# Reordering the recurrent mixer: solve ahead of the masks, operands of the second pair in the waits of the first, squares bank by bank, a new closing order

## The reference, cut to what matters

```python
def step(state, inp):
    r_t, w_t, k_t, v_t, kk_t, a_t = inp
    sa = jnp.einsum('bhvk,bhk->bhv', state, -kk_t)
    state = (state * w_t[:, :, None, :]
             + sa[..., None] * (kk_t * a_t)[:, :, None, :]
             + v_t[..., None] * k_t[:, :, None, :])
    return state, jnp.einsum('bhvk,bhk->bhv', state, r_t)
...
mean = jnp.mean(y, axis=-1, keepdims=True)
var = jnp.mean(jnp.square(y - mean), axis=-1, keepdims=True)
y = ((y - mean) * lax.rsqrt(var + GN_EPS)).reshape(B, S, RWKV_WIDTH) * ln_w + ln_b
...
y = y + bonus.reshape(B, S, RWKV_WIDTH)
return (y * g).astype(p_r.dtype)
...
x = x + jnp.concatenate([y_rw, y_pool], axis=-1) @ w_out[l]
```

## Time and profile before

| | us |
|---|---|
| median of 3 runs | 1474.83 |
| lowest and highest | 1473.97, 1476.49 |
| the profiled execution | 1472.81 |
| its span | 1471.0 |
| PE busy | 1426.8 (97%) |
| POOL, DVE, ACT busy | 778.8, 537.5, 504.5 |

### The profile page before, as it was taken

The page is one execution under the profiler, slowest core; times in us unless marked ns, Lnnn a source line. Parts: engine busy times, 40 slices in busy tenths (PEclk is TensorE's granted clock), DMA queues, the critical chain, the costliest instruction groups (busy, mean ns, idle before and its releaser), DMA issues.

```text
span 1471.0 us, 21748 instructions
## 1 busy us (share of the span) xinstructions
PE 1426.8 (97%) x8086; PEld 1172.9 (80%) x8086; DVE 537.5 (37%) x732; ACT 504.5 (34%) x709; POOL 778.8 (53%) x1028
## 2 busy tenths in 40 slices
PE   7999999999999999999999999989899999999997
PEld 5787888888888788888888867867688888888887
DVE  6986422222002842222200468964344222221003
ACT  5424433333213433232221466225443233232222
POOL 1663745555555855455555666563465545455553
PEclk9999999999999999999999999999999999999999
DMA  9882432223222322323332232200132322323321
GB/s 363 309 323 96 138 118 95 99 98 99 100 88 84 100 100 91 108 86 99 101 100 88 70 102 72 73 2 4 33 114 98 101 99 91 108 86 100 100 72 58
DMA packets 45705, 156.96 MB, mean 107 GB/s; under 512 B 5328, under 2 KB 8656, under 8 KB 45520
## 3 DMA queue, kind: packets, MB, share of 16 engines
q1 hardware_dynamic: 45648, 156.16, 30.9%
HBM read 154.04 MB, written 2.10 MB: 106 GB/s over the span
## 4 chain that ended last, share of the span: by engine, by line
PE 82%; DVE 10%; ACT 4%; issue 3%; POOL 1%; DMA 0%; DVEq 0%; SPq 0%; POOLq 0%; ACTq 0%
PE ps L1764 26%; PE ps L1766 26%; PE ps L1765 26%; POOL w_lo L543 1%; DVE tri_p L1191 1%; DVE tri_x L1191 1%; PE ps L2221 1%; DVE mid_sq L1194 1%; ACT w_hi L726 1%; DVE pads L1191 0%; DVE f_buf L1191 0%; DVE act_lo L1194 0%; DVE mod_acc L1194 0%; DVE rAR L1191 0%; PE ps L2279 0%
## 5 line engine op out<-in xcount | busy, mean ns | idle before, releaser
L543 POOL TENSOR_TENSOR w_lo<-raw,w_hi 128x256 fp32r<-128x256 f32 x932 | 694.3, 778 | 583.4 <-ACT w_hi L726 583.1
L1764 PE MATMUL ps<-act_hi,w_hi 128*128 128x512 f32 x1328 | 522.6, 393 | 8.2 <-POOL w_lo L543 3.5
L1766 PE MATMUL ps<-act_hi,w_lo 128*128 128x512 f32 x1328 | 517.1, 389 | 0.0
L1765 PE MATMUL ps<-act_lo,w_hi 128*128 128x512 f32 x1328 | 516.8, 389 | 0.0
L726 ACT ACTIVATE w_hi<-raw 128x1024 fp32r<-128x1024 f32 x233 | 244.7, 1054 | 432.8 <-PE ps L1766 402.4
L1764 PEld LDWEIGHTS ps<-act_hi,w_hi 128*128 128x128 f32 x1328 | 249.3, 188 | 67.4 <-POOL w_lo L543 4.8
L1766 PEld LDWEIGHTS ps<-act_hi,w_lo 128*128 128x128 f32 x1328 | 249.2, 188 | 52.3
L1765 PEld LDWEIGHTS ps<-act_lo,w_hi 128*128 128x128 f32 x1328 | 249.4, 188 | 52.0 <-issue 1.4
L1764 PE MATMUL ps<-hid_hi,w_hi 128*128 (+2 forms) x588 | 220.0, 374 | 0.8 <-issue 0.8
L1765 PE MATMUL ps<-hid_lo,w_hi 128*128 (+2 forms) x588 | 219.7, 374 | 0.0
L1766 PE MATMUL ps<-hid_hi,w_lo 128*128 (+2 forms) x588 | 219.7, 374 | 0.0
(11 more groups left out here) (281 smaller groups left out, 989.1 us busy)
## 6 DMA issues: line engine op xcount, KB each, us to landing
raw<-weight_units SPq DMA_DIRECT2D x233, 512.0 KB, 3.5
wm_mid<-mod_units SPq DMA_DIRECT2D x18, 512.0 KB, 8.6
wm_ring<-mod_units SPq DMA_DIRECT2D x14, 512.0 KB, 8.6
wm_early<-mod_units SPq DMA_DIRECT2D x8, 512.0 KB, 7.8
wm_late<-mod_units SPq DMA_DIRECT2D x8, 512.0 KB, 8.0
x_tok<-tokens SPq DMA_DIRECT2D x4, 512.0 KB, 6.5
xT<-tokens_by_channel SPq DMA_DIRECT2D x1, 2048.0 KB, 8.0
result<-act_out SPq DMA_DIRECT2D x16, 128.0 KB, 1.8
```

The lines of the kernel that those rows point to most:

```text
L543: ins = nc.gpsimd.tensor_tensor(w_lo[:, slot, c], raw[:, slot, c], w_hi[:, slot, c].bitcast(f32), SUB)
L1764: nc.tensor.matmul(o, wh, xh, start=start, stop=False, **check)
L1765: nc.tensor.matmul(o, wh, xl, start=False, stop=False, **check)
L1766: return nc.tensor.matmul(o, wl, xh, start=False, stop=stop, **check)
```

## The change

- **Solve.** All remaining steps of the solve and its transpose are issued on DVE before the front of pair 0. ACT copies all four blocks into `TT`, ahead of its copy `AVa`. The five filler products before G1 go; two stand before LR of pair 0.
- **First operands of pair 1.** A third letter, n, runs pieces of the next pair's front in stage 0: tV of pair 1 before W, tA of pair 1 before GH, with their copies on ACT. tV and tA are now two pieces. tV of pair 0 waits for 17 instead of 18 input units to be read. In stage 1 the front of pair 1 begins with K.
- **Blocks of the other pairs.** ACT's block copies are two pieces of two. In stages 2 and 3 the copy of state S0 stands between them.
- **Squares.** Y lies in two banks. DVE copies the half of the first bank (`y0`) while ACT squares the half of the second from PSUM (`sq1`), then they change banks (`y`, `sq`).
- **Closing.** ACT converts the first two output units and pool group 0 before the three finished pairs, and the third unit right behind them; DVE makes the low part of pool group 0 first; PE yields after each block and has one block between S5 and S6, one between S6 and Y, two between Y and var, and four between var and bc. POOL makes the low part of the third unit before the gate of pair 3.

```diff
-VE_STEPS = [..., "MT", "RP", "y", "inv", "yn"]
+VE_STEPS = [..., "MT", "RP", "y0", "y", "inv", "yn"]
...
+    fronts = [front(p) for p in range(PAIRS)] + [closing()]
     for s in range(PAIRS + 1):
-        turn = {"f": front(s) if s < PAIRS else closing()}
+        turn = {"f": fronts[s]}
         if s:
             turn["b"] = back(s - 1)
-        for who in order if s < PAIRS else last_order:
-            if who in turn:
-                next(turn[who], None)
+        if s == 0:
+            turn["n"] = fronts[1]
+        for who in orders[s]:
+            next(turn[who], None)
...
# POOL
             out_low("RO")
+            out_low("RO")
             gated(3)
-            out_low("RO")
             out_low("Y")
...
# ACT, front
                 copy("tV", b.VT[:, :], 0)
+                yield
                 copy("tA", b.AA[:, 0:2 * NCP, :], 1, "q (s k) -> q s k", k=HS)
-                if p:
-                    triangle_blocks(p)
+                yield
+                triangle_blocks(p, (0, 1))
+                yield
+                triangle_blocks(p, (2, 3))
                 yield
                 pe_did("AV")
                 did("AVa", ...)
-                if p == 0:
-                    triangle_blocks(p)
...
# ACT, back
-                ve_did("y")
-                did("sq", nc.scalar.activation(rK[:, p, :], rB[:, p, :], ACT.Square))
+                for name, o in (("sq1", 1), ("sq", 0)):
+                    if o:
+                        pe_did("Y")
+                    else:
+                        ve_did("y0")
+                    did(name, nc.scalar.activation(<half o of rK>, <half o of ps, banks of Y>, ACT.Square))
...
# ACT, closing: order of the pieces
-  N: high_n(U_OUT) | mix_hi(0) | mix_hi(1) | mix_hi(2) | pool_hi(0) | RO: high_n(U_OUT + 1) | pool_hi(1) | pool_hi(2) | pool_hi(3), high_n(U_OUT + 2), Y: high_n(U_OUT + 3)
+  N: high_n(U_OUT) | RO: high_n(U_OUT + 1) | pool_hi(0) | mix_hi(0) | mix_hi(1) | mix_hi(2) | high_n(U_OUT + 2) | pool_hi(1), pool_hi(2) | pool_hi(3), Y: high_n(U_OUT + 3)
-            in_stages(front, back, closing, "fbbbbfbbfbfbfbbf", "bfbbfbfbfbfbfbfbfbf")
+            in_stages(front, back, closing, ("fffffffnfnf", "ffbbbbfbbfbfbfbbf", "fffbfbbbfbbfbfbfbbf", "fffbfbbbfbbfbfbfbbf", "bfbfbfbfbfbfbfbfbbf"))
...
# DVE
-            solve_steps(1)
+            solve_steps(SB)
...
                 did("AVb", ...)
                 if p == 0:
-                    solve_steps(SB - 1 - SOLVED)
-                    solve_steps(1)
-                    after(sem("cleared"), cleared_through("TT0"))
-                    for e in (2, 3):
-                        triangle_block(nc.vector.tensor_copy, p, e)
                     bonus(0)
                     bonus(1)
...
-                pe_did("Y")
-                did("y", nc.vector.tensor_copy(<y>, <both banks of Y>))
+                for name, o in (("y0", 0), ("y", 1)):
+                    if o:
+                        ac_did("sq1")
+                    else:
+                        pe_did("Y")
+                    did(name, nc.vector.tensor_copy(<half o of y>, <bank o>))
...
# DVE, closing: order of the pieces
-  mix_lo(0), mix_lo(1) | mix_lo(2), pool_lo(0) | pool_lo(1) | pool_lo(2), pool_lo(3)
+  pool_lo(0), mix_lo(0) | mix_lo(1), mix_lo(2) | pool_lo(1), pool_lo(2) | pool_lo(3)
-            in_stages(front, back, closing, "bfbffffbfbfb", "bbffbfbfb")
+            in_stages(front, back, closing, ("fffffff", "bfbffffbfbfb", "bfbffffbfbfb", "bfbffffbfbfb", "bbffbfbfb"))
...
# PE
-            after(sem("in_read"), len(IN_ORDER))
...
                 if p >= 2:
                     pe.wait_ge(vector_step[p % 2], at(VE_STEPS, p - 2, "y"))
+                    pe.wait_ge(scalar_step[p % 2], at(AC_STEPS, p - 2, "sq"))
...
+                else:
+                    after(sem("in_read"), len(IN_ORDER) - 1)
...
                 did("tV", last)
+                yield
+                if p == 0:
+                    after(sem("in_read"), len(IN_ORDER))
...
                 ac_did("tA")
+                if p == 0:
+                    keep_busy(b.bank, 2)
...
                 ve_did("LR")
-                if p == 0:
-                    keep_busy(b.bank, 5)
                 ac_did("AVa")
...
-                for n, (m, k) in enumerate((m, k) for m in range(BEFORE_MIX) for k in others):
+                for m, k in ((m, k) for m in range(BEFORE_MIX) for k in others):
                     out_block(m, k, k == 0, False)
-                    if n % 2:
-                        yield
+                    yield
-            in_stages(front, back, closing, "fbfbbfbfbfbfbfbfbfb", "bbfbfbfbfbbbffbffb")
+            in_stages(front, back, closing, ("ffffffffnfnf", "fbbbfbfbfbfbfbfbfb", "ffbfbbfbfbfbfbfbfbfb", "ffbfbbfbfbfbfbfbfbfb", "bbfbfbfbfbfbfbffbffffb"))
```

More of the change, by code:

```diff
@@ L163 @@
             + [f"S{c}" for c in range(2, NCH - 1)] + ["Y", "var", "bc"])
-VE_STEPS = ["KA", "KR", "LR", "AVb", "G1b", "tK", "Wb", "GHb", "MT", "RP", "y", "inv", "yn"]
+VE_STEPS = ["KA", "KR", "LR", "AVb", "G1b", "tK", "Wb", "GHb", "MT", "RP", "y0", "y", "inv", "yn"]
 AC_STEPS = (["tV", "tA", "AVa", "G1a", "tB", "Wa", "GHa", "S0", "S1", "bias"] + [f"S{c}" for c in range(2, NCH - 1)]
-            + ["sq", "sd", "wide"])
+            + ["sq1", "sq", "sd", "wide"])
 PO_STEPS = ["X", "X next", "sum", "out"]
@@ L207, with in_stages @@
 LOW_FIRST = 5
-SOLVED = 29
-def in_stages(front, back, closing, order, last_order):
+def in_stages(front, back, closing, orders):
+    fronts = [front(p) for p in range(PAIRS)] + [closing()]
     for s in range(PAIRS + 1):
-        turn = {"f": front(s) if s < PAIRS else closing()}
+        turn = {"f": fronts[s]}
         if s:
             turn["b"] = back(s - 1)
-        for who in order if s < PAIRS else last_order:
-            if who in turn:
-                next(turn[who], None)
+        if s == 0:
+            turn["n"] = fronts[1]
+        for who in orders[s]:
+            next(turn[who], None)
         for who in ("b", "f"):
@@ L1015, in _, with triangle_blocks @@
             n_step = [0, 0]
-            def triangle_blocks(p):
+            def triangle_blocks(p, which):
                 b = sets[p % 2]
@@ L1023, in triangle_blocks @@
                     act.wait_ge(tensor_step[p % 2], at(PE_STEPS, p - 2, "GH"))
-                for e in range(2 if p == 0 else 4):
+                for e in which:
                     triangle_block(nc.scalar.copy, p, e)
@@ L1083, in back @@
                     yield
-                ve_did("y")
-                did("sq", nc.scalar.activation(rK[:, p, :], rB[:, p, :], ACT.Square))
+                for name, o in (("sq1", 1), ("sq", 0)):
[3 more added lines that the diff above has]
+                        ve_did("y0")
+                    did(name, nc.scalar.activation(rK[:, p, :].rearrange("q (c o t) -> q o c t", o=2, t=CH)[:, o, :, :],
+                                                   ps[:, b.bank + o, HALF:].rearrange("q (c t) -> q c t", t=CH), ACT.Square))
                 yield
@@ L1105, in closing @@
                 yield
+                act.wait_ge(tensor_step[1], at(PE_STEPS, PAIRS - 1, "RO"))
+                high_n(U_OUT + 1)
+                yield
+                pool_hi(0)
+                yield
                 act.wait_ge(pool_step[0], pool_at(PAIRS - 2, "out"))
@@ L1113, in closing @@
                 yield
-                pool_hi(0)
-                yield
-                act.wait_ge(tensor_step[1], at(PE_STEPS, PAIRS - 1, "RO"))
-                high_n(U_OUT + 1)
+                high_n(U_OUT + 2)
                 yield
                 pool_hi(1)
-                yield
                 pool_hi(2)
@@ L1667, in back @@
                 y = rB[:, p, :]
-                pe_did("Y")
-                did("y", nc.vector.tensor_copy(y.rearrange("q (c o t) -> q o c t", o=2, t=CH), by_half(0, HALF)))
+                for name, o in (("y0", 0), ("y", 1)):
[3 more added lines that the diff above has]
+                        pe_did("Y")
+                    did(name, nc.vector.tensor_copy(y.rearrange("q (c o t) -> q o c t", o=2, t=CH)[:, o, :, :], bank(o)[:, HALF:].rearrange("q (c t) -> q c t", t=CH)))
                 yield
@@ L1685, in closing @@
             def closing():
+                pool_lo(0)
                 mix_lo(0)
+                yield
                 mix_lo(1)
-                yield
                 mix_lo(2)
-                pool_lo(0)
                 yield
                 pool_lo(1)
+                pool_lo(2)
                 yield
-                pool_lo(2)
                 pool_lo(3)
-            in_stages(front, back, closing, "bfbffffbfbfb", "bbffbfbfb")
+            in_stages(front, back, closing, ("fffffff", "bfbffffbfbfb", "bfbffffbfbfb", "bfbffffbfbfb", "bbffbfbfb"))
             mix_lo(PAIRS - 1)
```

1 line of the change is left out of this document (removed).

## The result

| us | before | changed |
|---|---|---|
| median (lowest, highest) | 1474.40 (1472.22, 1476.49) | 1461.19 (1460.45, 1462.28) |
| the profiled execution | 1472.81 | 1462.28 |
| its span | 1471.0 | 1460.5 |
| PE busy | 1426.8 (97%) | 1424.0 (98%) |

The ratio is 0.9911, with the interval 0.9894 to 0.9928: faster by 13.2 us, where 10.3 were forecast. The two profiled executions are 10.5 apart, 0.2 more than the sum of the prediction. So the question is where the other 2.7 us come from.

What follows compares the result with a forecast made beforehand. PE, busy 97% of the span, was taken as the bound, so only its waits could be won. Terms 3.6 + 1.35 + 1.35 + 0.3 + 3.7 = 10.3 us gave 1474.8 - 10.3 = 1464.5 us, range 1461.5 to 1469.5.

Steps and rivals of the forecast that it cites:

- Masks at 968.5: Stage 0: sign that key masks of pair 0 start at 968.5, released by the solve hidden in DVE's 2.95 us idle time.
- G1 at 971.4: Stage 0: sign that G1 of pair 0 starts at 971.4 instead of 974.96, with no filler ahead.
- GH to S1 in 4.3: Pair 0: GH to S1 forecast at 4.36 us instead of 6.05, a gain of 1.7.
- var right behind W: Stages 1 to 3: sign that PE's var follows W with idle below 0.1 us, where it waited 0.51.
- the 2.91 wait gone and a smaller one on pool_lo(3) in its place: Closing: PE's 2.91 us wait on POOL's w_lo goes; a new one of about 1.6 comes on pool_lo(3).
- the solve: Stage 0: solve steps and transpose move ahead of the masks, so G1 comes 3.6 us earlier.
- the closing: Behind S5: new order starts the third unit's blocks at 61.05 instead of 64.79, a gain of 3.7 us.
- Part 3: Squares by bank start var 0.45 us earlier in three stages, 1.35; S0 between block copies gives 0.3; bounds 0.6 to 2.0.
- the reading of stage 3: Stage 3: clock at 0.91 over 18.78 us, a dip costing 1.7 us; gaps in PE's issue make the rest.
- Half of it comes: Rival, chance 0.25: stalls reappear as the next wait, above all in the closing; 5 to 7 us, about 1468.5.
- the last line of the sum: The runs' median lies 2.0 above the profiled execution, so the forecast is 1474.8 - 10.3 = 1464.5 us.
- The rival of the clock: Stage 3's dip removed, 1462.8 (0.1); dips added in stages 0 to 2, 1466 to 1468 (0.12); long low clock, 1479.5 (0.04).

Runs made afterwards that it cites:

- part 3 alone: Kernel before with only the squares by bank and S0 between the block copies; 1471.84 us, ratio 0.9987.
- first repetition: The changed kernel run again unedited, in more rounds; 1461.45 us, ratio 0.9923 to the kernel before.
- part 1 alone: Kernel before with only the solve moved ahead of the masks, four blocks on ACT, two fillers instead of five; 1469.48 us, ratio 0.9977.
- part 2 alone: Kernel before with only tV and tA of pair 1 in pair 0's waits and K before MT; 1471.44 us, ratio 0.9985.
- part 4 alone: Kernel before with only the closing's new order on ACT, DVE, PE and POOL, old copy and square of Y; 1469.20 us, ratio 0.9973.
- POOL's line alone: Kernel before with only POOL's low part of the third output unit ahead of pair 3's gate; 1468.82 us, ratio 0.9973.
- before, stall filled: Kernel before with three filler products in the 2.9 us wait ahead of the third output unit; 1472.19 us, ratio 0.9991.
- changed, gate back: Changed kernel with POOL's gate of pair 3 back ahead of the third unit's low part; 1465.67 us, ratio 0.9957 to before.
- changed, no fillers: Changed kernel without its two filler products ahead of LR of pair 0; 1464.62 us, ratio 0.9938 to before.
- changed, pool group 3 early: Changed kernel with the fourth pool group's conversions one piece earlier on ACT and DVE; 1459.40 us, ratio 0.9913, again 1459.63, ratio 0.9902, to before.
- the same, one product earlier: Changed kernel with pool group 3 early, and the first pool product moved between N and S1 of the last stage; 1461.61 us, ratio 0.9920 to before.

## Why the prediction was right, and where it failed

**The mechanisms held, and all sizes but one.** Masks at 968.5, G1 at 971.4, GH to S1 in 4.3, var right behind W, the 2.91 wait gone and a smaller one on pool_lo(3) in its place: all five as written. In the table the largest miss of a term is 0.22, in the solve: G1 comes as forecast, but the end of the last input unit, from which the stretch is counted, came 0.19 sooner. The last solve step took 0.34 beside POOL's copies, not 0.19; the earlier start of the solve absorbed it. The bounds on the closing (1.5 to 4.8) were far wider than needed. Part 3 was sized too small, and that its row fits is luck. Without the gaps in PE's issue it gained 2.1, just above its bound of 2.0, and more gaps took 0.6 of it. These gaps aren't only scatter. From S1 of pair 0 to S1 of pair 3 they sum to 0.35 to 1.11 us in the nine traces of kernels that square Y whole, and to 1.29 to 1.91 in the nine with the squares by bank (part 3 alone 1.91): about 1 us more in the mean, which the prediction put at nothing. What makes them is open. Nor does the reading of stage 3 close: it needed 3.4 us from dip and gaps, and the row of the dip gives 1.7 and the trace one gap of 0.90. "Half of it comes" is refuted: in the closing no stall came back beyond the one named.

**The step that failed** is the last line of the sum: "The median of the runs lies 2.0 above it, so the forecast is 1474.8 - 10.3". It takes the distance between the profiled execution and the median for something that belongs to the kernel and outlives the change. In the changed kernel the median lies 1.1 below its profiled execution instead (1461.19 against 1462.28), so the term was -1.1 where +2.0 was added. That makes 3.1 of the 3.3 us between forecast and result; the rest is the sum, 10.5 instead of 10.3. The distance is low clock. Of the 78 executions of before, the 22 with a mean granted clock of 0.997 or more average 1471.35 us, the 51 at 0.995 or less 1475.11. The profiled one was of the first kind (one low stretch, at 0.997), the median is of the second kind (the two of these that were traced, at 0.993 and 0.994, have a loss of four and of three such stretches). The changed kernel's executions at 0.997 or more average 1461.35. The mean clock also holds the end of the span, where PE has no work left and the low level costs nothing, so 0.997 stands for one stretch or none; a window of the changed kernel:

```profile
1455.00:1460.00 5.00, 0.00 (x0) 0.00 (x0) 2.64 (x7) 0.00 (x0) 0.00 (x0) 0.50 0.63 210
```

Its profile has one stretch (at 1004) and took 1462.28, that of its first repetition has none and took 1460.72: 1.56 apart, about the price of one. The two profiled executions lie 1.5 and 0.9 above the mean of their kind, so that their difference, 10.5, comes near that of the kinds is in part luck.

Compared at the same clock the change brings 1471.35 - 1461.35 = 10.0, near the forecast's 10.3. The means over all executions are 1473.86 at 0.9951 and 1461.64 at 0.9971: 12.2 apart, of which the clock has 0.0020 x 1474 = 2.9, enough for the 2.2 left over. So the changed kernel runs 10 us faster by its order of work, and some 2 to 3 by losing one or two low stretches per execution.

**What removed them** is settled only in part. The rival of the clock named the right thing with the wrong place and sign: it priced the dip seen in stage 3 and feared more in stage 0. The dips that went are those that the profiled execution didn't have. The clocks of all versions:

| version | stall of 2.9 | mean clock | executions at 0.997 or more |
|---|---|---|---|
| before | yes | 0.9951 | 22 of 78 |
| part 1 alone (solve) | yes | 0.9961 | 2 of 11 |
| part 2 alone (operands of pair 1) | yes | 0.9960 | 2 of 12 |
| part 3 alone (squares) | yes | 0.9960 | 7 of 12 |
| part 4 alone (closing) | no | 0.9957 | 4 of 12 |
| POOL's line alone | no | 0.9966 | 8 of 12 |
| before, stall filled | 1.0 left | 0.9963 | 8 of 12 |
| changed | no | 0.9971 | 12 of 13 |
| changed, gate back | yes | 0.9958 | 3 of 5 |
| changed, no fillers | no | 0.9948 | 0 of 6 |
| changed, pool group 3 early | no | 0.9975 | 9 of 11 |
| the same, one product earlier | no | 0.9968 | 2 of 5 |

Two sources of low clock are seen. The stall of 2.9 has it at its end in five of eight traces, and putting the stall back costs 4.3 us, of which 3.1 are in the stretch. The unfilled wait of 2.26 in stage 0 has it 1.6 us behind its end in the one trace taken, and no execution without the fillers reaches 0.997. But the stall isn't the only source that went: parts 1 to 3 keep it and still have a higher clock than before, and part 4 takes it away and gains no more than they. Why the whole change reaches 0.9971, which no part alone does, is open. So is the share of each part in the 2 to 3 us: each part alone has an interval of 1.6 to 2.0 us on either side, and the four (3.4, 2.2, 1.9 and 4.0 by their ratios, 11.5 in sum) can't be told from terms with or without their share. By their medians they would be 5.2, 2.9, 2.8 and 5.5, 16.3 in sum and more than the whole change brings: the median of before stands among the executions of low clock, and with each part alone many executions leave that group. Nor do the runs show why a given execution gets the low level at a given place.

## What to carry to other kernels

Before adding a profiled sum to a median, look at the clock of every run: compare executions at the same mean granted clock, and price the difference between them apart. Here a PE wait of 2 to 3 us cost its length and, in part of the executions, 1.7 us more behind it, so such waits go first, and where one can't go a filler product in it can be worth more than it seems. And when a stall is moved to another conversion (here 1.29 on the fourth pool group), ask once more whether that conversion's inputs are ready earlier: here they were, and it was worth 1.6.

## What the runs showed of the hardware that was not expected

- The granted clock falls to 1.2 GHz also inside stretches of small products with no wait over 1 us. In the changed kernel's profile it does so 2 us behind a gap of 0.92 in PE's issue, as in that of before, at 1028.9, behind one of 0.90; the windows are its timeline cut at the fall and the rise:

```profile
1000.00:1004.50 4.50, 3.14 (x96) 2.56 (x90) 1.81 (x3) 1.28 (x4) 0.00 (x0) 0.99 0.02 4
1004.50:1008.00 3.50, 3.50 (x41) 2.72 (x33) 0.69 (x1) 0.91 (x2) 0.00 (x0) 0.52 0.00 0
1008.00:1017.91 9.91, 9.69 (x256) 8.19 (x255) 5.25 (x9) 6.15 (x14) 2.55 (x2) 1.00 0.02 4
```

- PE's issue gaps without any wait (0.15 to 1.03 us; 0.92 at 1001.90 in the changed kernel) come in runs of many 64x64 products, mostly in the same few runs but with other lengths in each execution: 1.11 us in sum before, 1.71 and 1.55 in two profiles of the changed kernel. A part's gain of 1.5 us has to be read against them, and they can rise with a change of order, as above with the squares by bank.
- The last solve step took 0.34 beside POOL's copies, and the step before it, of the same width, 0.19. The low part of a finished pair (act_lo, 128x512) took 0.80, 0.86 and 0.92 at 1038.92 to 1041.09 in the changed kernel, while POOL made w_lo in pieces of 0.81, and 0.69 in two of its variants at 1052.8, also while POOL made w_lo. At 1052.8 it was POOL that paid: its four pieces took 3.29 in the variant with pool group 3 early, where four took 2.80 at 1042.47 in the changed kernel. The Trainium skill (SBUF — State Buffer, "SBUF: two separate sides") has the shared port as held by one engine for a whole instruction. These rows agree in kind. In size they show less than that: an act_lo of 0.69 cost POOL 0.49 there, and none of the three above is longer by more than 0.23.
